# Key pages of the sample attention transposed on VectorE instead of TensorE

## What is computed

```python
# q (8, 8, 8 heads, 128); k_sel, v_sel: the batch's 256 past rows of each head
ls = einsum('bqhd,bqhsd->bqhs', q, k_sel) * 128 ** -0.5 + bias(distance)
lo = einsum('bqhd,bkhd->bqhk', q, k_new) * 128 ** -0.5 + bias(distance)
p = softmax(concat([ls, where(causal, lo, -1e30)]))
out = p[..., :256] @ v_sel + p[..., 256:] @ v_new
```

## Time and profile before

| | |
|---|---|
| median of 3 runs | 1634.09 us (1632.97 to 1634.69) |
| profiled execution | 1633.22 us |
| its span, first to last instruction | 1631.5 us |
| TensorE busy | 1610.1 us (99%) |
| VectorE busy | 1037.3 us (64%) |
| ScalarE busy | 627.6 us (38%) |
| GpSimd busy | 225.9 us (14%) |
| HBM traffic over the span | 156 GB/s |

### The profile page before, as it was taken

One profiled execution on the slowest core, in us unless ns is written; L12 is line 12 of the kernel. 1 busy time (PEld: TensorE's weight loads), 2 busy tenths in 40 slices (PEclk: granted clock), 3 DMA queues, 4 the chain that ended last, 5 costly groups with the idle time before them and its releaser, 6 DMA issues.

```text
span 1631.5 us, 30727 instructions
## 1 busy us (share of the span) xinstructions
PE 1610.1 (99%) x12847; PEld 1571.0 (96%) x12847; DVE 1037.3 (64%) x1651; ACT 627.6 (38%) x794; POOL 225.9 (14%) x354
## 2 busy tenths in 40 slices
PE   7999999999999999999999999999999999999997
PEld 7999989999999999999999999999999999999997
DVE  5675688557444555776656576666666666666666
ACT  6553334323443343733333333333333333333334
POOL 1122322223112121310000000000000101010004
PEclk9999999999999999999999999999999999999999
DMA  8444453446655566445444544445444444444442
GB/s 247 138 143 132 136 162 111 130 137 227 213 168 202 183 201 206 145 142 154 155 149 148 154 145 154 148 146 158 145 155 145 152 152 146 155 145 153 142 156 85
DMA packets 230954, 255.59 MB, mean 157 GB/s; under 512 B 9412, under 2 KB 220934, under 8 KB 230816
## 3 DMA queue, kind: packets, MB, share of 16 engines
q1 hardware_dynamic: 217856, 220.12, 43.8%
q0 software_dynamic: 10272, 32.24, 5.7%
q10 hardware_dynamic: 2688, 1.27, 0.3%
HBM read 242.48 MB, written 12.69 MB: 156 GB/s over the span
## 4 chain that ended last, share of the span: by engine, by line
PE 94%; DVE 4%; DMA 1%; issue 1%; ACT 0%; SPq 0%; DVEq 0%; POOLq 0%; POOL 0%
PE ps_proj L1823 23%; PE ps_proj L1825 22%; PE ps_proj L1824 22%; PE ps_small L1823 6%; PE ps_small L1825 6%; PE ps_small L1824 6%; PE ps_small L1865 2%; DVE w_lo L1209 1%; DVE conv_acc L1252 1%; DMA x_raw<-in_x_sample_dram 0%; PE ps_small L2103 0%; PE ps_proj L1865 0%; PE ps_small L2199 0%; PE ps_small L2217 0%; PE ps_small L1998 0%
## 5 line engine op out<-in xcount | busy, mean ns | idle before, releaser
L1823 PE MATMUL ps_proj<-x_hi,w_hi 128*128 128x320 f32 x2432 | 763.1, 314 | 1.0 <-issue 0.7
L1825 PE MATMUL ps_proj<-x_hi,w_lo 128*128 128x320 f32 x2432 | 751.8, 309 | 0.0
L1824 PE MATMUL ps_proj<-x_lo,w_hi 128*128 128x320 f32 x2432 | 751.5, 309 | 0.0
L840 ACT ACTIVATE w_hi<-w_raw 128x1024 fp32r<-128x1024 f32 x408 | 431.8, 1059 | 718.0 <-PE ps_proj L1825 522.3
L1209 DVE TENSOR_TENSOR w_lo<-w_raw,w_hi 128x1024 fp32r<-128x1024 f32 x408 | 497.6, 1223 | 304.5 <-ACT w_hi L840 304.0
L1823 PEld LDWEIGHTS ps_proj<-x_hi,w_hi 128*128 128x128 f32 x2432 | 457.0, 188 | 11.8 <-issue 8.9
L1824 PEld LDWEIGHTS ps_proj<-x_lo,w_hi 128*128 128x128 f32 x2432 | 457.2, 188 | 0.3
L1825 PEld LDWEIGHTS ps_proj<-x_hi,w_lo 128*128 128x128 f32 x2432 | 456.8, 188 | 0.0
L1823 PE MATMUL ps_small<-hid_hi,w_hi 128*128 128x320 f32 x704 | 217.5, 309 | 0.0
L1825 PE MATMUL ps_small<-hid_hi,w_lo 128*128 128x320 f32 x704 | 217.1, 308 | 0.0
L1824 PE MATMUL ps_small<-hid_lo,w_hi 128*128 128x320 f32 x704 | 217.0, 308 | 0.0
(11 more groups left out here) (351 smaller groups left out, 1154.7 us busy)
## 6 DMA issues: line engine op xcount, KB each, us to landing
w_raw<-in_w_up_dram SPq DMA_DIRECT2D x176, 512.0 KB, 3.5
w_raw<-in_w_in_dram SPq DMA_DIRECT2D x112, 512.0 KB, 4.1
w_raw<-in_w_down_dram SPq DMA_DIRECT2D x88, 512.0 KB, 3.5
w_raw<-in_w_out_dram SPq DMA_DIRECT2D x32, 512.0 KB, 3.7
k_pages<-in_cache_k_dram POOLq DMA_DIRECT2D x32, 256.0 KB, 3.7
v_pages<-in_cache_v_dram POOLq DMA_DIRECT2D x32, 256.0 KB, 4.5
state_s<-in_state_gdn_dram POOLq DMA_DIRECT2D x8, 512.0 KB, 6.0
out_ss_dram<-state_s POOLq DMA_DIRECT2D x8, 512.0 KB, 3.8
```

Of the source, the lines that this page charges most:

```text
L840: act.activation(whi[:, slot], raw[:, slot], ACT.Copy).then_inc(hi_done, 1)
L1823: pe.matmul(o, hi, rhs_hi[:, k0 + kk_, :], start=first and kk_ == 0, stop=False)
L1824: pe.matmul(o, hi, rhs_lo[:, k0 + kk_, :], start=False, stop=False)
L1825: ins = pe.matmul(o, lo, rhs_hi[:, k0 + kk_, :], start=False, stop=last and kk_ == CQ - 1)
```

## The change

In the sample attention, `P kt` and `A kt` are gone. The keys are transposed by VectorE in blocks of 32x32, one instruction of 128x1024 for each batch (`V kt`), from `k_pages` to `k_t_blocks`. For that, GpSimd brings each page by two DMAs of 64 rows, so that each 32 rows of the tile hold 32 positions. After the transposes, 32 partitions hold 32 of the 128 key dimensions for these positions, and the four parts of the dimensions lie beside each other. The queries are copied by ScalarE into `q_rep0` and `q_rep1` so that each 32 partitions have each 32 dimensions (`A qr`, 16 copies for each half `q`). An `SS` step now takes two batches: for each of four dimension parts, four heads and four row groups one product of 32x32 by 128 columns, summed over the dimension parts, into four banks. A query is multiplied with the keys of both batches and of the other batches as well; `V SS` picks its own by four passes, each with a mask (`ownscale`) that holds the scale or zero. `q_z` is gone. The banks of `PT` and `OT` change. In the list of steps the sample part is written anew, and the table of lengths changes for other steps too (`kv`, `S`, `E`, `N`, `PT`, `ab`, `gs`), which moves steps that are otherwise the same. The core of the diff:

```diff
@@ -67,6 +67,7 @@
     parts["own"] = own
+    parts["ownscale"] = np.where(own, SCALE, 0.0)
...
@@ -246,25 +247,17 @@
         s += [("P", "O", g, h), ("A", "O", g, h)]
-    s += [("P", "kt", g, 0), ("G", "qz", g), ("A", "kt", g, 0), ("V", "kt", g, 0), ("V", "qz", g, 0)]
-    soft = []
-    for q in range(2):
-        for b in range(4 * q, 4 * q + 4):
-            s += [("P", "SS", g, b)]
-            if b < DB - 2:
-                s += [("G", "pk", g, b + 2)]
-            s += soft[:1]
-            if b < DB - 1:
-                s += [("P", "kt", g, b + 1)] + soft[1:3] + [("A", "kt", g, b + 1), ("V", "kt", g, b + 1)]
-            soft = soft[3:]
-            if b == 3:
-                s += [("V", "SS", g, 0), ("V", "qz", g, 1), ("A", "SE", g, 0), ("V", "SN", g, 0)]
-                soft = [("P", "PT", g, 0), ("A", "PT", g, 0), None,
-                        ("P", "PV", g, 0), ("A", "PV", g, 0), None,
-                        ("P", "OT", g, 0), ("A", "OT", g, 0), None]
-            s = [x for x in s if x]
-            if ("P", "PV", g, 0) in s and ("G", "pv", g, 4) not in s:
-                s += [("G", "pv", g, 4 + j) for j in range(4)]
+    s += [("G", "qz", g), ("A", "qr", g, 0, 0), ("A", "qr", g, 0, 1)]
+    soft = {2: [("P", "PT", g, 0), ("A", "PT", g, 0), ("P", "PV", g, 0), ("A", "PV", g, 0), ("P", "OT", g, 0), ("A", "OT", g, 0)]
+               + [("G", "pv", g, 4 + j) for j in range(4)]}
+    for p in range(DB // 2):
+        for b in (2 * p, 2 * p + 1):
+            s += [("V", "kt", g, b)] + ([("G", "pk", g, b + 2)] if b < DB - 2 else [])
+        if p == 2:
+            s += [("V", "SN", g, 0)]
+        s += [("P", "SS", g, p)] + soft.get(p, [])
+        if p == 1:
+            s += [("V", "SS", g, 0), ("A", "qr", g, 1, 0), ("A", "SE", g, 0), ("A", "qr", g, 1, 1)]
...
@@ -282,11 +275,11 @@
           "os": 12, "ot": 6, "gs": 7,
-          "ks": 9, "us": 12, "sh": 11, "kv": 12, "S": 11, "O": 12, "kt": 10, "hb": 6, "SS": 6, "PT": 4, "PV": 16, "OT": 2, "ab": 30},
-    "A": {"sc2": 25, "sc5": 24, "ab": 10, "qs": 15, "nc": 8, "pl": 8, "o": 10, "oq": 3, "kv": 16, "E": 14, "SE": 9, "gs": 10, "kt": 8, "PT": 9, "fp": 22},
+          "ks": 9, "us": 12, "sh": 11, "kv": 9, "S": 9, "O": 12, "hb": 6, "SS": 13, "PT": 2, "PV": 16, "OT": 2, "ab": 22},
+    "A": {"sc2": 25, "sc5": 24, "ab": 10, "qs": 15, "nc": 8, "pl": 8, "o": 10, "oq": 3, "kv": 8, "E": 4, "SE": 9, "gs": 15, "qr": 16, "PT": 9, "fp": 22},
     "V": {"sc1": 11, "sc3": 50, "sc4": 15, "ss": 0, "gt": 5, "dm": 15, "dc": 1, "kk": 20, "kq": 9, "tk": 0, "bv": 0,
           "o2": 13, "oz": 1, "dx": 15, "dh": 4, "df": 17, "dg": 6, "ks": 8, "st": 0, "oc": 18, "o1": 0, "um": 0, "us": 33, "hk": 8,
-          "S": 16, "N": 9, "SS": 15, "SN": 7, "kt": 8, "hb": 12, "qz": 3},
+          "S": 18, "N": 4, "SS": 23, "SN": 7, "kt": 22, "hb": 12},
...
@@ -534,18 +527,19 @@
     ktp_at = a.at
-    ktp = a.put("k_t_past", [P, 4, 2 * P])
+    a.put("k_t_past", [P, 4, 2 * P])
     bm = nc.alloc_sbuf_tensor_at("bias_q", [P, 4, 2 * P], F32, offset=ktp_at)
...
     pt = a.put("probs_t", [P, 2, 384])
-    qz = nc.alloc_sbuf_tensor_at("q_z", [P, 4 * (P + DT)], F32, offset=pt_at)
     kp = a.put("k_pages", [P, 2, 2, 4, P])
     vp_at = a.at
     vp = a.put("v_pages", [P, 4, 2, 4, P])
     ob = a.put("o_tok", [P, P])
-    ast = a.put("att_small", [P, 2, 8])
+    ast = small[:, 640:656].rearrange("p (a b) -> p a b", a=2)
+    qr = [nc.alloc_sbuf_tensor_at("q_rep0", [P, 4, 4, BLK], F32, offset=pt_at), a.put("q_rep1", [P, 4, 4, BLK])]
+    kT = nc.alloc_sbuf_tensor_at("k_t_blocks", [P, 2, (ktp_at - work_at) // 4], F32, offset=work_at)
...
@@ -999,9 +993,15 @@
                     finish(act.activation(reg[g][:, h, 0:SEQ], b3[:, 0:SEQ], ACT.Copy))
-                elif name == "kt":
-                    after(act, "P", "kt", *k)
-                    finish(act.activation(ktp[:, :, 0:P], heads(b0, P), ACT.Copy))
+                elif name == "qr":
+                    g, q, half = k
+                    after(act, "A", "O", g, 3)
+                    if g:
+                        after(act, "P", "SS", 0, 3)
+                    for i in (2 * half, 2 * half + 1):
+                        for d in range(4):
+                            ins = act.activation(qr[q][32 * i:32 * i + 32, d], reg[g][32 * d:32 * d + 32, 0:4, SEQ + 32 * q:SEQ + 32 * q + 32], ACT.Copy)
+                    finish(ins)
...
@@ -1568,22 +1568,26 @@
                 elif name == "kt":
-                    after(dve, "P", "kt", *k)
-                    finish(dve.tensor_copy(ktp[:, :, P:2 * P], heads(b1, P)))
-                elif name == "qz":
-                    g, q = k
-                    after(dve, "G", "qz", g)
-                    if q:
-                        after(dve, "P", "SS", g, 3)
-                    finish(dve.tensor_copy(diagonal(qz), reg[g][:, 0:4, SEQ + 32 * q:SEQ + 32 * q + 32]
-                                           .rearrange("p h (j t) -> p j h t", j=4)))
+                    g, b = k
+                    dve.wait_ge(pk_in[b % 2], 64 * (DB // 2 * g + b // 2 + 1))
+                    if b == 0:
+                        after(dve, "A", "O", g, 3)
+                        for i in range(2):
+                            dve.wait_ge(kv_out[i], 32 * ((2, 1), (3, 3))[g][i])
+                    elif b > 1:
+                        after(dve, "P", "SS", g, b // 2 - 1)
+                    finish(dve.transpose(kT[:, b % 2, 0:1024], kp[:, b % 2].rearrange("p i h d -> p (i h d)")))
                 elif name == "SS":
                     g, q = k
-                    after(dve, "P", "SS", g, 4 * q + 3)
+                    after(dve, "P", "SS", g, 2 * q + 1)
                     after(dve, "V", "hb", g)
                     o_ = 2 * P + 32 - 32 * q
-                    dve.scalar_tensor_tensor(out=sc[:, q, 0:256], in0=b2[:, 0:256], scalar=SCALE, in1=bs[:, 0:256],
-                                             op0=ALU.mult, op1=ALU.add)
+                    past, total = (ap.rearrange("p (a x) -> p a x", a=4) for ap in (sc[:, q, 0:256], bs[:, 0:256]))
+                    for j in range(4):
+                        at = CONST_COLS["ownscale"][0] + j
+                        chain(dve.scalar_tensor_tensor(out=past, in0=psB[:, 0:4, 64 * j:64 * j + 64],
+                                                       scalar=cst[:, at:at + 1], in1=total, op0=ALU.mult, op1=ALU.add))
+                        total = past
...
@@ -2171,41 +2175,34 @@
                     finish(ins)
-                elif name == "kt":
-                    g, b = k
-                    pe.wait_ge(pk_in[b % 2], 32 * (DB // 2 * g + b // 2 + 1))
-                    if b == 0:
-                        after(pe, "A", "O", g, 3)
-                    else:
-                        after(pe, "A", "kt", g, b - 1)
-                        after(pe, "V", "kt", g, b - 1)
-                    for i, bank in ((0, b0), (1, b1)):
-                        for h in range(4):
-                            ins = turn(bank[:, h * P:(h + 1) * P], kp[:, b % 2, i, h, :], P)
-                    finish(ins)
                 elif name == "SS":
-                    g, b = k
-                    q, j = b // 4, b % 4
-                    after(pe, "A", "kt", g, b)
-                    after(pe, "V", "kt", g, b)
-                    if j == 0:
-                        after(pe, "V", "qz", g, q)
+                    g, p = k
+                    q, half = p // 2, p % 2
+                    after(pe, "V", "kt", g, 2 * p + 1)
+                    if p == 3:
+                        after(pe, "A", "OT", g, 0)
+                    if half == 0:
+                        after(pe, "A", "qr", g, q, 1)
                         if q:
...
                                       reg[g][:, 4 + h, SEQ:TOK], start=True, stop=True)
-                    for h in range(4):
-                        ins = pe.matmul(b2[32 * h:32 * h + 32, 0:256], qz[:, P * j + 32 * h:P * j + 32 * h + 32], ktp[:, h, :],
-                                        start=j == 0, stop=j == 3, skip_group_check=True)
+                    keys = kT[:, :, 0:1024].rearrange("p s (i h d) -> p s i h d", i=2, h=4)
+                    for d in range(4):
+                        for h in range(4):
+                            for i in range(4):
+                                rows = slice(32 * i, 32 * i + 32)
+                                ins = pe.matmul(psB[32 * h:32 * h + 32, i, P * half:P * half + P], qr[q][rows, d, h, :],
+                                                keys[rows, :, :, h, 32 * d:32 * d + 32], start=d == 0, stop=d == 3)
                     finish(ins)
...
                     after(pe, *(("A", "OT", k[0], 0) if q else ("A", "O", k[0], 3)))
-                    turn(b3[:, 0:P], sc[:, q, 0:P], P)
-                    turn(b3[:, P:2 * P], sc[:, q, P:2 * P], P)
-                    finish(turn(b3[0:NS, 2 * P:3 * P], sc[:, q, 2 * P:TOK], P))
+                    turn(b0[:, 256:384], sc[:, q, 0:P], P)
```

(7 more changed lines are left out.)

## The result

The change makes the kernel slower: 1668.97 us median (1667.19 to 1671.45) beside 1634.11 of the kernel before on the same chip (1632.97 to 1634.69), ratio 1.0216 with a 95% interval of 1.02 to 1.0232. The profiled execution took 1667.22 us, its span is 1665.5. The forecast was 1619.5, and 1629 was the top of its range.

A forecast was written before the change was run, and what follows sets the result against it. TensorE, busy 99%, was taken to bound the kernel. Profiled 1633.2 us, less 15.2 saved (25.6 of old steps minus 10.4 of new), plus 0.6 of waits, is 1618.6; with 0.9 to the median 1619.5, range 1615 to 1629.

The forecast's parts named there:

- The step that failed: GpSimd issues 32 page DMAs more at about 0.54 us each, bytes and packets unchanged; it idles.
- the prediction's check of chunk 98: Tightest VectorE queue in sample attention: pages there at 6.7 us, `lo_part(101)` done at 9.9, wanted at 11.8, margin 1.9.
- Score steps of 1.30 us, bounds 1.19 to 1.55: New TensorE cost in sample attention: eight steps of 64 products at 1.30 us each, 10.4 us in all.
- a sign of being wrong: The forecast is wrong if a new score step on TensorE costs above 2 us.
- the forecast saving: TensorE in sample attention: 25.6 us of old steps less 10.4 us of new ones, 15.2 us saved.
- The u step: Existing TensorE step at 366.07, eight products of the same form in two tiles, 1.19 us: lower end for a score step.
- the `dx` step: Existing TensorE step, 32 products of 32x32 in 0.88 us; read as issuing, it gave the score step's upper end, 1.55.
- C: Rival: row groups of one column strip do not work together; score steps 4.0 us each, 1641 us; chance 0.07.
- D: Rival: VectorE's float32 block transposes are slow, above 2.1 us each; at 4.4 us each 1644 us; chance 0.05.
- E: Rival: nothing gained, within 0.2% of before, from 25 ns per record or handover waits at their worst; chance 0.05.
- B: Rival: shortened lengths pack steps too tightly to cover handovers; 3 to 10 us come back, 1624 to 1631 us; chance 0.14.
- the 0.6 us of waits: TensorE waiting at head 3's transpose `T` under the new lengths, 0.3 us per group; bounds none to 3 us.

The follow-up runs named there:

- the halved step: The change with one 128-row DMA per page, score steps doing two of the four head-dimension parts, 32 products for 64: 1620.29 us, a step 1.20.
- whole pages: The change with one DMA of 128 rows per page as before, bias and scaled scores put in order on VectorE: 1628.54 us, ratio 0.9975 to before.
- light weights: Weight chunks 94 to 143 loaded as 32 KB instead of 512 KB: 1626.58 us on whole pages, 1643.05 us on the change, one execution each.
- turned loops: Whole pages with the four heads as innermost loop of a score step: 1628.49 us, a step 2.03.
- moved value products: Whole pages with score transposes and value products of each group's first half moved to just before its last score step: 1629.17 us, ratio 0.9973 to before.

## Why the prediction was wrong

**The step that failed** is one sentence among those on the other engines: the 32 further page DMAs were costed at nothing, "the bytes stay and the packets too, since a row of 2 KB is one packet either way". That was taken from the size of a row, not from a trace; no row of before had such a source. The rows do stay as they were; the runs showed 224 further packets of 8 bytes for each DMA of 64 rows, landing in 7.3 us where the prediction's check of chunk 98 used 3.7, and issues of 0.67 us for 0.54. With 7.3 "the pages are there at 6.7" becomes 10.3, past the whole margin of 1.9 us. The split pages alone cost the kernel before 46 us, and taking them out of the change won back 40. None of the rivals was this one. Why such packets make pages land late stays open.

**Score steps of 1.30 us, bounds 1.19 to 1.55.** That the tiles run together was right, the size was not: 2.03, outside both bounds and over the 2 us that the prediction had named as a sign of being wrong, so 8 x 0.73 = 5.8 us of the forecast saving are missing. The u step fills two tiles with 16 records, so it shows streaming and hides issuing; the `dx` step shows issuing and hardly streaming. I took the one nearer in form and treated the other as an alternative, when they add: 1.19 for the first and 64 x 13 ns = 0.83 for the issuing are 2.02, in this step at least.

**The other rivals.** C did not come: in turn, 64 products would have cost 4.0 us. Nor did D: the transposes, taken at 1.22, took 1.24. E did not come: 128 records in 1.90 us are 15 ns each. The rule of the Trainium skill, "TensorE: Matmul & The Clock Gate", section "Back-to-back issue gap", can't be taken for each record here. For each product it is near what the halved step shows, 0.83 us for 32, or 26 ns; but with 64 columns a product takes (0.415 - 0.107) / 16 us = 19 ns, so that in this kernel it is no floor either.

**The lengths** (B and the 0.6 us of waits) went the other way. No wait at a transpose of `scores` or a `T` step is to be seen with whole pages, and there the old lengths cost 10 us. They had been worked through for collisions only, not for what the old ones would do.

**What the prediction had no term for** is TensorE's own instructions. The sum with whole pages comes out: 1619.5 + 5.8 for the score steps, + 1.57 + 0.87 for two stops at late instructions, + 1.81 for the value step that ScalarE's DMA issues held up, - 0.6 for waits that did not come, is 1629.0; measured 1628.5. So even without the late pages the time would have been at the very top of the range, and for reasons that the prediction did not have.

Open: what the 8-byte packets are, how far ahead instructions are asked for, and what in the traffic holds a transfer back, were not tried. That late instructions cause the stops rests on the times of the transfers, on the run with half of the products and on one execution with light weights.

## What to carry to other kernels

When a DMA's source or destination pattern changes, the same bytes are no evidence of the same packets: count the packets and the landing time in the first trace, above all where a ring of few slots makes the landing part of a cycle. Price a burst of small products in many tiles as streaming and issuing added. And read a stop of TensorE that no semaphore explains together with the queue that carries instructions: here bursts of short products used them up fast, and full DMA engines brought them late. A wait that does name another engine may still be the same fault at one remove: look at what that engine stood before in its own order.

The version with whole pages is faster than both kernels, 0.25% below before. The turned loops and the moved value products give the same time.

## What the runs showed of the hardware

A DMA of GpSimd's queue with 64 consecutive rows of 2 KB moved as 32 packets of 4096 bytes and 16 of 4 bytes; one whose 64 rows are two runs of 32 with a step between them had 224 packets of 8 bytes more. Its issue took 671 ns beside 524 for 64 consecutive rows and 497 for 32, and it landed in 7.3 us beside 3.6 and 3.7. Sixteen tiles of 32x32 in float32 run together, but a round of 128 columns takes 0.415 us, 0.213 of it streaming. TensorE's instructions come in 16 KB transfers over the same DMA engines as data, 101 of them before and 107 after on queue 8, which is one for 256 records, and in 17 of 20 stops TensorE went on 1.2 to 1.6 us after a late one had ended. Leaving out 94% of the weight bytes in the stretch made the kernel hardly faster (1626.6 in one execution beside 1628.5 us).
